# Transformer and state-space blocks on one core: weights split inside the output streams, rows right behind the root, three units at once behind each norm

## The reference, cut to what matters

```python
for i in range(2):
    mod, mod_c = silu(c) @ ada_w[i] + ada_b[i], silu(c_ctx) @ ada_w[i] + ada_b[i]
    h, hc = modulate(x, norm_mix_g[i], sh1, sc1), modulate(ctx, ..., csh1, csc1)
    y, yc = attention_mixer(h, hc, ...) if i == 0 else ssm_mixer(h, hc, ...)
    x = x + g1 * y
    x = x + g2 * swiglu(modulate(x, norm_ffn_g[i], sh2, sc2), gate, up, down)
    # ctx likewise while i == 0
return rmsnorm(x, final_norm_g)
```

## Time and profile before

| what | value |
|---|---|
| median of 3 runs | 1677.86 us (1676.86 to 1682.76) |
| the profiled execution | 1676.07 us, of which the span of instructions is 1674.2 us |
| mean granted TensorE clock | 0.946 of full |
| busy: TensorE, its weight loads, VectorE, ScalarE, GpSimd | 93%, 77%, 45%, 36%, 12% |
| HBM read | 202.76 MB, 123 GB/s over the span |

### The profile page before, as it was taken

One profiled execution on the slowest core, in us unless ns is written; L12 is line 12 of the kernel. 1 busy time (PEld: TensorE's weight loads), 2 busy tenths in 40 slices (PEclk: granted clock), 3 DMA queues, 4 the chain that ended last, 5 costly groups with the idle time before them and its releaser, 6 DMA issues.

```text
span 1674.2 us, 22685 instructions
## 1 busy us (share of the span) xinstructions
PE 1557.3 (93%) x9424; PEld 1288.7 (77%) x9424; DVE 746.9 (45%) x1208; ACT 599.3 (36%) x1126; POOL 206.0 (12%) x195
## 2 busy tenths in 40 slices
PE   7999999897979988999999998799999899899997
PEld 6887799574835566788888886578898688699996
DVE  6761125315146733423322332776754762255453
ACT  4342344224225633422122222542344460253342
POOL 2000384011000001011001102000000130111021
PEclk9799999797979999999999999899999898899998
DMA  7313554854200014122323231222352242645451
GB/s 231 139 51 126 198 187 162 322 222 187 101 1 1 26 50 159 68 93 91 132 76 101 69 121 61 101 99 85 119 178 74 97 157 79 230 170 188 176 172 43
DMA packets 36109, 206.84 MB, mean 124 GB/s; under 512 B 4952, under 2 KB 9480, under 8 KB 14888
## 3 DMA queue, kind: packets, MB, share of 16 engines
q1 hardware_dynamic: 33344, 200.11, 33.1%
q10 hardware_dynamic: 1848, 2.52, 0.8%
q0 software_dynamic: 816, 2.78, 0.5%
HBM read 202.76 MB, written 2.62 MB: 123 GB/s over the span
## 4 chain that ended last, share of the span: by engine, by line
PE 83%; DVE 6%; ACT 5%; DMA 3%; issue 1%; POOL 1%; SPq 1%; ACTq 0%; POOLq 0%; DVEq 0%
PE lin L1647 18%; PE lin L1648 17%; PE lin L1649 17%; PE lin L1630 7%; PE lin L1753 3%; PE aux L1982 2%; PE modp L1679 2%; DMA ring<-ada_in 2%; PE lin L2005 1%; PE lin L2160 1%; PE aux L1988 1%; ACT hn_hi L671 1%; ACT hn L672 1%; PE aux L1695 1%; PE aux L2077 1%
## 5 line engine op out<-in xcount | busy, mean ns | idle before, releaser
L592 DVE TENSOR_TENSOR w_split<-ring,w_split 128x1024 fp32r<-128x1024 f32 (+1 forms) x140 | 187.0, 1339 | 383.3 <-ACT w_split L587 383.2
L587 ACT ACTIVATE w_split<-ring 128x1024 fp32r<-128x1024 f32 (+1 forms) x140 | 158.4, 1134 | 479.4 <-PE lin L1649 402.5
L1647 PE MATMUL lin<-hn_hi,w_split 128*128 128x512 f32 (+1 forms) x864 | 304.7, 353 | 13.9 <-DVE hn_lo L879 11.9
L1649 PE MATMUL lin<-hn_hi,w_split 128*128 128x512 f32 (+1 forms) x864 | 301.1, 348 | 0.0
L1648 PE MATMUL lin<-hn_lo,w_split 128*128 128x512 f32 (+1 forms) x800 | 276.6, 346 | 0.0
L1647 PEld LDWEIGHTS lin<-hn_hi,w_split 128*128 128x128 f32 x864 | 165.0, 191 | 41.8 <-DVE hn_lo L879 12.0
L1649 PEld LDWEIGHTS lin<-hn_hi,w_split 128*128 128x128 f32 x864 | 165.7, 192 | 20.4
L1648 PEld LDWEIGHTS lin<-hn_lo,w_split 128*128 128x128 f32 x800 | 153.7, 192 | 16.8
L1647 PE MATMUL lin<-hn_hi,w_split_ssm 128*128 128x512 f32 (+2 forms) x392 | 135.0, 345 | 14.2 <-DVE w_split_ssm L592 8.0
L1648 PE MATMUL lin<-hid_split,w_split 128*128 128x512 f32 (+1 forms) x416 | 143.2, 344 | 0.0
L1648 PE MATMUL lin<-hn_lo,w_split_ssm 128*128 128x512 f32 (+2 forms) x392 | 133.9, 342 | 0.0
(11 more groups left out here) (376 smaller groups left out, 2562.0 us busy)
## 6 DMA issues: line engine op xcount, KB each, us to landing
ring<-ada_in SPq DMA_DIRECT2D x48, 1024.0 KB, 4.9
ring<-ssm_in_in SPq DMA_DIRECT2D x24, 1024.0 KB, 4.8
ring<-od_in_in SPq DMA_DIRECT2D x12, 1024.0 KB, 4.9
ring<-ffn0a_in_in SPq DMA_DIRECT2D x11, 1024.0 KB, 6.4
ring<-ffn0b_in_in SPq DMA_DIRECT2D x11, 1024.0 KB, 4.8
ring<-ffn1a_in_in SPq DMA_DIRECT2D x11, 1024.0 KB, 4.9
ring<-ffn1b_in_in SPq DMA_DIRECT2D x11, 1024.0 KB, 4.8
ring<-ev_in_in SPq DMA_DIRECT2D x9, 1024.0 KB, 13.5
```

The source lines that it names most:

```text
L587: act.activation(parts[:, 0], w, ACT.Copy).then_inc(sig("w_high"), 1)
L592: dve.tensor_tensor(parts[:, 1], w, parts[:, 0].bitcast(F32), ALU.subtract).then_inc(sig("w_low"), 1)
L1647: mm(lin[0:m, tile % RING, 0:width], hi, x_hi, start=kt == 0, stop=False)
L1649: ins = mm(lin[0:m, tile % RING, 0:width], lo, x_hi, start=False, stop=kt == kts - 1)
```

## The change

- `STREAM`: two `qkv` blocks go ahead of the last two of `od_out`; two `ffn1a_in` blocks go ahead of the last two of `ssm_out`.
- The low parts of `qkv` units 0 to 3 move from behind the `od_out` additions to between them; those of `ffn1a_in`, high and low, into the `ssm_out` stream. `ffn0a_in` unit 3 moves from ahead of the last addition of `w_o` to behind it.
- TensorE does `ada(3)` ahead of the sums, spreads the root at once, and does the fourth block after that. ScalarE's copy of the group moves behind the shifts, and `ada_groups` behind unit 3 of the product.
- The first three units after a norm (for norm 4: `ssm_dt`, `ssm_in` 0 and 1) are taken together, kt by kt, in three banks.
  The dots below stand for the three matmuls of one unit at one kt.
- `w_split_ssm` gets a third place; high parts of `ssm_in` run at n + 4, low parts at n + 5, the latter behind `convolve(n)` where n + 2 stood ahead of it.

```diff
+def split_together(units, x, width, waits):
+    for name, u, m in units:
+        begin("lin", lin_of[name] + u)
+        pe.wait_ge(sig("w_low"), unit_of[name] + u + 1)
+    for kt in range(KT):
+        pe.wait_ge(sig("hn_ready"), waits + kt + 1)
+        x_hi, x_lo = x(kt)
+        for name, u, m in units:
+...
 # split_linear
+                first = 0
+                if norm is not None:
+                    first = 3
+                    split_together([(name, u, P) for u in range(first)], x, width, KT * norm)
+                for u in range(first, dict(SPLIT)[name]):
                     split_unit(name, u, kts, x, width, waits=waits if u == 0 else None)
+                    if u == 3 and later is not None:
+                        later()
 # TensorE, feed_forward (norm 2 likewise)
-                ada(2)
-                norm(k, width, between=lambda: ada(2))
-                ada_groups(7 if n == 0 else 11)
+                ada(3)
+                norm(k, width)
+                ada(1)
 # STREAM
-("od_out", 4), ("qkv", 2), ("ada", 4)
+("od_out", 2), ("qkv", 2), ("od_out", 2), ("ada", 4)
-("ssm_out", KT), ("ffn1a_in", 2), ("ada", 4)
+("ssm_out", 6), ("ffn1a_in", 2), ("ssm_out", 2), ("ada", 4)
 # ScalarE, norm 4 and ssm_in
                 weights_hi(act, "ssm_in", 0)
+                weights_hi(act, "ssm_in", 1)
             act_norm(act, 4, 2 * L, "ffn0b_out", (1, 0, 2), True, first_weights)
-            weights_hi(act, "ssm_in", 1)
             weights_hi(act, "ssm_in", 2)
+            weights_hi(act, "ssm_in", 3)
...
-                if n + 3 < 48:
-                    weights_hi(act, "ssm_in", n + 3)
+                if n + 4 < 48:
+                    weights_hi(act, "ssm_in", n + 4)
 # VectorE, norm 4 and ssm_in
-            modulated(dve, own, 4, 2 * L, 1, 0, 2)
-            weights_lo(dve, "ssm_in", 1)
+            modulated(dve, own, 4, 2 * L, 1, 0, 2, lambda: weights_lo(dve, "ssm_in", 1))
+            weights_lo(dve, "ssm_in", 2)
...
-            convolve(dve, own, 0)
-            convolve(dve, own, 1)
+            for n in range(2):
+                convolve(dve, own, n)
+                weights_lo(dve, "ssm_in", n + 5)
...
-            for n in range(2, 46):
-                weights_lo(dve, "ssm_in", n + 2)
+            for n in range(2, 43):
                 if n < 32:
                     convolve(dve, own, n)
+                weights_lo(dve, "ssm_in", n + 5)
```

More of the change, by code:

```diff
@@ L576, in unit @@
             first, memory, places_, shift = chain(name)
[L577 removed]
+            place = (unit_of[name] + u - unit_of[first] + shift) % places_
+            parts = memory[place][:, :, 0:cols] if first == "ssm_dt" else memory[:, place, :, 0:cols]
             return parts, ring[:, b % RING, u % per_block * cols:(u % per_block + 1) * cols], b
@@ L642, in ada_copies, with act_norm @@
                 act.activation(ada_sb[:], modp[:, 0:L], ACT.Copy).then_inc(sig("ada_copied"), 1)
-        def act_norm(act, k, width, after=None, shift=None, split=False, meanwhile=None, before=None, later=None):
+        def act_norm(act, k, width, after=None, shift=None, split=False, meanwhile=None, before=None, later=None, last=None):
             for kt in range(KT):
@@ L660, in act_norm @@
                   tile)
-            if later is not None:
+            if shift is None and later is not None:
                 ada_copies(act, later, 1)
@@ L1592, in _, with query_weights @@
             modulations(dve, own, 0, 6)
-            add_to_x("od_out")
+            def query_weights(n):
+                if n % 2 == 0 and n < 4:
+                    for u in (n, n + 1):
+                        weights_lo(dve, "qkv", u)
+            add_to_x("od_out", query_weights)
             second_block_vector(dve, own)
@@ L1610, in linear @@
             def linear(name, stage, tiles, kts, rhs, width=L, m=P, norm=None, ready=None):
[L1612 to L1618, removed]
+                for n, b in enumerate(blocks_of[name]):
+                    pe.wait_ge(w_in[b % RING], (b // RING + 1) * 16)
                     for j in range(tiles):
[L1620 to L1623, removed]
+                        tile = lin_of[stage] + n * tiles + j
+                        begin("lin", tile)
@@ L1631, in one @@
+                            ins = mm(lin[0:m, tile % RING, 0:width], ring[:, b % RING, at:at + m], rhs(kt),
                                      start=kt == 0, stop=kt == kts - 1)
                         fills(ins, "lin")
-                rounds(pe, count, one)
+            def split_together(units, x, width, waits):
[6 more added lines that the diff above has]
+                    for name, u, m in units:
+                        parts, _, _ = unit(name, u)
+                        hi, lo = (parts[:, part, kt * m:(kt + 1) * m] for part in range(2))
+                        out = lin[0:m, (lin_of[name] + u) % RING, 0:width]
+                        mm(out, hi, x_hi, start=kt == 0, stop=False)
+                        mm(out, hi, x_lo, start=False, stop=False)
+                        ins = mm(out, lo, x_hi, start=False, stop=kt == KT - 1)
+                        if kt == KT - 1:
+                            fills(ins, "lin")
@@ L1951, in _ @@
             both = slice(0, 2 * L)
-            ada(2)
-            norm(2, 2 * L, between=lambda: ada(2))
-            ada_groups(6)
-            split_linear("qkv", KT, lambda kt: (hn_hi[:, kt, :], hn_lo[:, kt, :]), 2 * L, ("hn_ready", KT * 2))
+            ada(3)
+            norm(2, 2 * L)
+            ada(1)
+            split_linear("qkv", KT, lambda kt: (hn_hi[:, kt, :], hn_lo[:, kt, :]), 2 * L,
+                         later=lambda: ada_groups(6), norm=2)
             pe.wait_ge(sig("at_in"), 48)
@@ L2040, in _ @@
             norm(4, 2 * L)
-            split_unit("ssm_dt", 0, KT, lambda kt: (hn_hi[:, kt, :], hn_lo[:, kt, :]), 2 * L, 2 * M_HEADS,
-                       ("hn_ready", KT * 4))
-            for tile in range(48):
+            split_together([("ssm_dt", 0, 2 * M_HEADS), ("ssm_in", 0, P), ("ssm_in", 1, P)],
+                           lambda kt: (hn_hi[:, kt, :], hn_lo[:, kt, :]), 2 * L, KT * 4)
+            for tile in range(2, 48):
                 width = 2 * L if tile < 24 else L
```

83 lines of the change are left out of this document (51 added, 32 removed).

## The result

| | before | changed |
|---|---|---|
| median of 4 runs | 1678.54 us (1676.86 to 1682.76) | 1661.78 us (1657.23 to 1664.43) |
| the profiled execution, its span | 1676.07, 1674.2 us | 1664.43, 1662.6 us |
| mean granted TensorE clock | 0.946 | 0.955 |

The ratio is 0.9891, with a 95% interval of 0.9869 to 0.9913. The prediction was 1665.0 with a range of 1651 to 1674. The ratio says 18.3.

The account below looks back on a forecast made before the run. TensorE was taken as the bound (83% of the chain, 93% busy), with waits around norms and at the head of `ssm_in`. 14.2 + 6.7 + 7.5 - 16.3 = 12.1 us off 1677.86 gave 1665.8, stated as 1665, range 1651 to 1674.

Parts of the forecast that it names:

- Norm 2: At norm 2, split and loads leave the path, scaling begins at 383.9 instead of 394.6, unit 3 sooner: gain 14.2 us.
- the three together: First three units behind norm 2, 72 matmuls: 11.7 at low clock, 60.3 at 0.227 us, together 18.7 us.
- the 5 us of low clock: Assumed slow-clock stretch as the first three units start after a norm; without it norm 2 would gain 2.4 us more.
- Norm 3: At norm 3, unit 3 comes 8.8 us sooner, less a new 2.1 us TensorE stall ahead of unit 4: net 6.7 us.
- norm 5: At norm 5, unit 3 comes 9.6 us sooner, less the same 2.1 us stall: net 7.5 us.
- Norm 4 and `ssm_in`: Stage from norm 4 through `ssm_in`: loss of 16.3 us, about 3 at the head and 13 at the narrow units.
- The series of four steps: In each `ssm_in` round, convolution, Silu, high part and low part run in series: 5.18 us wide, 4.2 us narrow.
- a wait of six microseconds ahead of unit 4: Sign at `ssm_in`: TensorE waits six microseconds for L1002, as unit 4 needs unit 0's bank, freed by the first convolution.
- Late blocks of `od_out` and `ssm_out`: Moved stream blocks, asked for later, land at least 1 us before they are needed; priced at nothing.
- That the head costs little: Rival at `ssm_in`: head and narrow rounds overlap, only 3 us lost, gain 25, giving 1653 us; chance 0.17.
- That the clock falls in each narrow round: Rival at `ssm_in`: narrow units take 5.1 instead of 4.2 us, 7.6 more, giving 1673 us; chance 0.10.
- That the three stay at the low clock: Rival at the norms: first three units run slow throughout, 41 us more, giving 1707 us; chance 0.05.

Follow-up runs that it names:

- the old head: Changed kernel with norm 4 and `ssm_in` put back as before the change: 1644.2 us, ratio to before 0.9795.
- the nearer low part: Changed kernel with the `ssm_in` low part of n + 4, not n + 5, behind convolution n: 1640.0 us, ratio to before 0.9759.
- the group moved: Changed kernel with `ada_groups` right behind the first three units, ahead of unit 3, in norms 2, 3 and 5: 1655.3 us, ratio to before 0.9858.
- the three versions with both mends: Changed kernel with low part n + 4 and `ada_groups` ahead of unit 3: 1633.7 us; plus convolutions 0, 1 early: 1629.2; plus high part behind root: 1626.8.

## Why the prediction was right

**Norm 2: +14.2 predicted, +17.5 measured.** The way there was right (split and load off the path, rows at once). The term that was off is the three together, put at 18.7: they took 16.45, because no slow stretch came; the prediction had put 2.4 on that. The rest is 0.75 of an earlier start and 0.14 of the group. The windows of the changed kernel show the three in norm 2, then in norm 3 and norm 5, then `ssm_dt` and its two:

```profile
390.00:398.00 8.00, 8.00 (x36) 6.60 (x37) 7.16 (x15) 8.00 (x21) 0.00 (x0) 1.00 0.79 326
...
655.20:661.00 5.80, 5.80 (x23) 4.66 (x20) 5.44 (x12) 5.80 (x15) 0.00 (x0) 0.71 1.01 428
...
1453.00:1457.00 4.00, 3.91 (x33) 3.94 (x34) 3.94 (x10) 4.00 (x11) 0.00 (x0) 1.00 0.99 412
...
1030.00:1034.00 4.00, 3.91 (x10) 2.76 (x11) 3.67 (x8) 4.00 (x12) 0.00 (x0) 0.50 1.01 428
```

Full, low in part, full, low: the 5 us of low clock taken for all four held for two of them. Which way it goes in norm 2 is luck. Of the seven traces with the changed order there (the changed kernel, the old head, the nearer low part, the group moved, and the three versions with both mends) five have the three in 16.4 us and two in 17.9.

**Norm 3: +6.7, measured +7.4; norm 5: +7.5, measured +10.2.** In norm 3 each step held: start at 10.9 after the stream, 18.0 for the three, stall 2.3. In norm 5 the three took 8.7 instead of 10.9 at a full clock.

**Norm 4 and `ssm_in`: -16.3, measured -15.7.** The series of four steps in each round was read out of the code and priced from rows: 4.2 a narrow round, measured 4.15; a wait of six microseconds ahead of unit 4, measured 5.77; low parts waiting 1.6 for ScalarE, measured 1.43. Counted from the end of the three, T, units 10, 24 and 36 were put at T + 61.3, 137.4 and 185.5; they began at T + 61.0, 137.2 and 184.8. Moving one line by one unit took the series away, which shows the cause. The sum left the clock at full. It fell in the head and at unit 27, but VectorE's chain set the head's times, so this moved little: the waits there were only shorter by what the matmuls took longer. That the narrow waits show 1.02 where 1.3 was predicted is no miss, since the round grew by 1.27.

**Late blocks of `od_out` and `ssm_out`.** They cost nothing: the `ssm_out` stream takes 55.35 us in both traces (1393.79 to 1449.14, 1390.95 to 1446.30), `od_out` 27.8 in both, without a wait for a load. The caution drawn from the Trainium skill (DMA: Bandwidth & Descriptors, "Two DMAs through the same engine are not ordered") did not come to bear here.

**The sum.** 12.1 predicted, 19.4 by these stages, 17 to 18 by the times. Of the 7.3 us between the first two, 3.3 lie in norm 2, 2.7 in norm 5, 0.7 in norm 3 and 0.6 at norm 4 and `ssm_in`; some 4.5 of them are the slow stretch that the sum took into the three of norms 2 and 5 and that did not come. What the other stages gave or took between the two profiled executions (mainly 3.4 us ahead of `od_out` and 4.6 from `qkv` to `w_o`, both against the changed kernel) was not predicted. It looks like variation: `od_out` begins anywhere from 347.2 to 352.9 us in the ten kernels with the same code ahead of it, and from `qkv` unit 3 to the first unit of `w_o` the traces take 189.3 to 196.2 us, the kernel before 189.3 and the changed one 192.7. No run here isolated what varies.

**The rivals.** That the head costs little was wrong, by the 16 us. That the clock falls in each narrow round was wrong (1.00 from 1205 to 1236); it fell once, at unit 27, which took 4.46 us where 2.88 is the full-clock time. That late blocks cost was wrong, as said. That the three stay at the low clock was wrong: in norms 3 and 4 it lasted some 3 to 4 us of them.

## What to carry to other kernels

When a step is moved further ahead, write out for each engine's queue what now stands in front of it; a low part made one unit later in the same round cost 22 us here, because four short operations on two engines came to stand in series. Early splits, early loads and the order of the matmuls that use them are one edit: the sum over the parts, each taken out alone, was 49 us where all of them give 40, and the new order without the early splits made the sums of norm 2 start 4 us later than before. Three units at once, fed kt by kt, gave 13 us, and that with the stall of 2.2 ahead of unit 4 still there, both with them and singly; letting the group through first, for which VectorE waits, gave another 4.5. And a wait's price is read from the distance of the starts, with it and without it, not from the idle time shown: 1.27 us, not 1.02, in each narrow round here.

## What the runs showed of the hardware

The clock fell around the longer waits of TensorE at `ssm_in` and not around the short ones. Behind 5.77 us at unit 4 the next 4 us had a clock of 0.50, behind 2.82 at unit 8 the stretch had 0.68, behind 2.04 at unit 27 it had 0.73. Behind 1.75 at unit 9 it was 1.00 (1106 to 1110), and seven waits of 1.02 us in 31 us, with TensorE busy 24.30 of them, left it at 1.00. Behind a wait of 2.52 that follows the rows of norm 2 both happened with the same code ahead of it: 1.00 in one execution and 0.60 in another. At unit 27, where TensorE set the pace, the fall cost some 1.5 us (4.46 instead of 2.88); in the head, where VectorE's chain set it, unit 10 still came at T + 61.0 instead of the T + 61.3 of a sum without it.
The Trainium skill (TensorE: Matmul & The Clock Gate, "A second HAM failure mode: psum-queue depth-cycling") says that small idle spells between groups, as banks are cycled through, make the clock swing. The seven short waits, 4.15 us apart, don't show it here; what the trace shows are single falls, behind the waits of 2.04 and 2.82 us.
